# Six modulation pairs of two column strips each in place of twelve single units

## The reference, cut to what matters

```
mod_lat = silu(c) @ w_mod + b_mod          # w_mod: 1024 x 6144
mod_ctx = silu(c_ctx) @ w_mod + b_mod
sh1, sc1, g1, sh2, sc2, g2 = split(mod_lat, 6)
prj_c = modulate(rmsnorm(ctx), sh1c, sc1c) @ w_in
prj_l = modulate(rmsnorm(x),   sh1,  sc1)  @ w_in
...
x = x + g1 * mix_l
x = x + g2 * hier_moe(modulate(rmsnorm(x), sh2, sc2), ...)
```

## Time and profile before

| what | us |
|---|---|
| median of three runs | 1448.57 |
| the runs | 1447.49, 1448.57, 1452.31 |
| span of the profiled execution, first to last instruction | 1448.4 |
| TensorE busy in it | 1317.8 (91%) |
| VectorE busy | 800.7 (55%) |
| ScalarE busy | 612.3 (42%) |
| GpSimd busy | 85.0 (6%) |

### The profile page before, as it was taken

One profiled execution on the slowest core, in us unless ns is written; L12 is line 12 of the kernel. 1 busy time (PEld: TensorE's weight loads), 2 busy tenths in 40 slices (PEclk: granted clock), 3 DMA queues, 4 the chain that ended last, 5 costly groups with the idle time before them and its releaser, 6 DMA issues.

```text
span 1448.4 us, 26402 instructions
## 1 busy us (share of the span) xinstructions
PE 1317.8 (91%) x11218; PEld 1122.8 (78%) x11218; DVE 800.7 (55%) x1221; ACT 612.3 (42%) x952; POOL 85.0 (6%) x65
## 2 busy tenths in 40 slices
PE   7999999999999999999999999899978767877877
PEld 7989798999989988899998999688545333444534
DVE  5557846776467676877548797785212111221314
ACT  6553346434466676455446654764211111111112
POOL 2000000000002200321001000320000000000000
PEclk9999999999999999999999999999999998999999
DMA  9654346454474585444554060349999999999996
GB/s 372 245 210 182 117 175 274 188 202 180 175 289 177 188 326 227 190 175 175 188 204 200 2 253 12 161 168 382 403 427 427 430 428 429 428 427 429 425 428 269
DMA packets 30358, 383.31 MB, mean 265 GB/s; under 512 B 3552, under 2 KB 3728, under 8 KB 7216
## 3 DMA queue, kind: packets, MB, share of 16 engines
q1 hardware_dynamic: 29504, 377.72, 64.3%
q0 software_dynamic: 752, 4.11, 0.7%
HBM read 380.77 MB, written 1.05 MB: 264 GB/s over the span
## 4 chain that ended last, share of the span: by engine, by line
PE 55%; DMA 25%; DVE 11%; ACT 5%; issue 2%; SPq 0%; POOL 0%; DVEq 0%; ACTq 0%; POOLq 0%
PE ps L688 55%; DMA ring<-in_experts 25%; DVE w_lo L2002 3%; DVE work L2014 2%; ACT work L1453 2%; ACT w_hi L1453 2%; DVE work L2002 1%; DVE HM L2002 1%; ACT L1453 1%; DVE act L2002 1%; ACT HM L1453 1%; ACT act L1453 0%; DVE HM L2008 0%; DVE work L2281 0%; PE ps L837 0%
## 5 line engine op out<-in xcount | busy, mean ns | idle before, releaser
L2002 DVE TENSOR_TENSOR w_lo<-ring,w_hi 128x1024 fp32r<-128x1024 f32 (+1 forms) x273 | 342.0, 1262 | 209.5 <-ACT w_hi L1453 209.0
L688 PE MATMUL ps<-in_hi,w_hi 128*128 128x256 f32 x1376 | 391.2, 284 | 15.0 <-DVE w_lo L2002 14.1
L688 PE MATMUL ps<-in_hi,w_lo 128*128 128x256 f32 x1376 | 387.3, 281 | 0.0
L688 PE MATMUL ps<-in_lo,w_hi 128*128 128x256 f32 x1376 | 387.0, 281 | 0.0
L1453 ACT ACTIVATE w_hi<-ring 128x1024 fp32r<-128x1024 f32 (+1 forms) x273 | 286.3, 1053 | 234.1 <-PE ps L688 230.4
L688 PE MATMUL ps<-ring,work 128*32 128x256 f32 (+3 forms) x2520 | 201.3, 452 | 85.5 <-DMA ring<-in_experts 77.7
L688 PEld LDWEIGHTS ps<-in_hi,w_hi 128*128 128x128 f32 x1376 | 261.5, 190 | 20.4 <-issue 16.6
L688 PEld LDWEIGHTS ps<-in_lo,w_hi 128*128 128x128 f32 x1376 | 261.5, 190 | 0.3
L688 PEld LDWEIGHTS ps<-in_hi,w_lo 128*128 128x128 f32 x1376 | 261.4, 190 | 0.0
L688 PEld LDWEIGHTS ps<-ring,work 128*32 128x32 f32 (+1 forms) x2520 | 83.8, 117 | 185.8 <-issue 103.8
L2014 DVE SCALAR_TENSOR_TENSOR X<-ps,mod,X 128x256 f32<-128x256 f32 x136 | 59.0, 479 | 249.4 <-PE ps L688 249.3
(11 more groups left out here) (291 smaller groups left out, 1904.0 us busy)
## 6 DMA issues: line engine op xcount, KB each, us to landing
ring<-in_experts SPq DMA_DIRECT2D x89, 2048.0 KB, 23.1
ring<-in_dense SPq DMA_DIRECT2D x82, 2048.0 KB, 7.7
ring<-in_experts SPq DMA_DIRECT2D x5, 512.0 KB, 21.5
work<-in_experts SPq DMA_DIRECT2D x1, 2048.0 KB, 12.6
ring<-in_dense SPq DMA_DIRECT2D x3, 512.0 KB, 7.4
spare<-in_experts SPq DMA_DIRECT2D x1, 1536.0 KB, 10.9
cst<-in_ret_cst POOLq DMA_DIRECT2D x1, 1280.0 KB, 12.6
cst<-in_experts SPq DMA_DIRECT2D x1, 1280.0 KB, 5.7
```

Of the source, the lines that this page charges most:

```text
L688: i = pe.matmul(o, l, r, start=start, stop=stop)
L2002: i = dve.tensor_tensor(out=o, in0=x, in1=y, op=op)
```

## The change

The twelve units become six pairs (`MOD_GROUPS`). A pair's 16 matmuls go to the four strips of one bank: unit one to strips 0 and 1, unit two to strips 2 and 3, each strip summing four input blocks. The order alternates so that four matmuls in a row go to strips 0, 1, 2, 3. Both units must have landed before the first matmul; the first unit's slot is released near the pair's end. ScalarE reads one bank per pair. A fold is again four matmuls, each with four moving columns (two per unit), so it serves both units.

The first pair (units 0 and 1) is done at the retention's end, with its fold now between the two halves of head 3's transposes. Pairs 1, 2 and 4 are at the starts of `ffn_in0`, `lru_u` and `ffn_in1`. Nothing is left inside the recurrent gates; pair 3 follows them, with its fold behind the first unit of `lru_out`. Pair 5 is at `ctx_b`. The stream of loads is put in the same order. With six tiles fewer, the bank of each later tile is counted anew, and the expert stage takes its bank numbers from the tiles.

```diff
-STREAM = [("ret_g", 0, 4), ("ret_v", 0, 4), ("ret_q", 0, 2), ("ret_k", 0, 2), ("mod", 0, 1), ("ret_out", 0, 4),
-          ("mod", 1, 2), ("ffn_in0", 0, 11), ("ffn_out0", 0, 6), ("mod", 3, 2), ("lru_u", 0, 3), ("lru_y", 0, 3),
-          ("lru_gate", 0, 1), ("mod", 5, 1), ("lru_gate", 1, 1), ("mod", 6, 2), ("lru_out", 0, 3), ("mod", 8, 2), ("ffn_in1", 0, 11),
+STREAM = [("ret_g", 0, 4), ("ret_v", 0, 4), ("ret_q", 0, 2), ("ret_k", 0, 2), ("mod", 0, 2), ("ret_out", 0, 4),
+          ("mod", 2, 2), ("ffn_in0", 0, 11), ("ffn_out0", 0, 6), ("mod", 4, 2), ("lru_u", 0, 3), ("lru_y", 0, 3),
+          ("lru_gate", 0, 2), ("mod", 6, 2), ("lru_out", 0, 3), ("mod", 8, 2), ("ffn_in1", 0, 11),
...
+MOD_GROUPS = (0, 1), (2, 3), (4, 5), (6, 7), (8, 9), (10, 11)
...
 for _i in range(KL):
-    if _i == KL // 2:
-        _mod(5)
     _seq.append(("lru_gate", _i))
-_mod(6, 7)
+_mod(3)
...
-GATHER_BANK, Y_BANK = 2, 4
-SCATTER_BANKS = 5, 6, 7, 3
+GATE_BANK, UP_BANK, GATHER_BANK, _last = (TILE["t_tok", i] % ROT for i in range(4))
+Y_BANK = GATHER0[1]
+SCATTER_BANKS = GATHER0[0], STAT, MODB, _last
...
+            def mod_rows(group):
+
+                units = MOD_GROUPS[group]
+                w = weights("mod", units[0]), ring[SLOT[UNIT_AT["mod", units[1]]]]
+                await_unit(pe, UNIT_AT["mod", units[1]])
+                if group == 0:
                     pe.wait_ge(s["csil_ready"], 1)
+                t = TILE["mod", group]
                 await_room(pe, t)
+                for first in range(0, KD, 2):
+                    for n in range(2):
+                        for c in (first, first + 1):
+                            rows = slice((2 * n + c % 2) * STRIP, (2 * n + c % 2 + 1) * STRIP)
+                            mm(bank(t)[rows, :], csil[:, c, :], w[n][:, c * 512:(c + 1) * 512], c < 2, c >= KD - 2,
+                               bank_full[t % ROT] if n and c == KD - 1 else None)
+                        if n == 0 and first == KD - 2:
+                            left.append(slot_used[SLOT[UNIT_AT["mod", units[0]]]])
...
+                to = cut(ps[:, MODB, 8 * units[0]:8 * (units[0] + 2)], 2, 8)
+                fold = cut(col("fold", 0, 4), 2, 2)
                 for m in range(4):
+                    mm(to[:, :, 2 * m:2 * m + 2], act2[:, group % 2, m * P:(m + 1) * P], fold, True, True,
                        s["mod_full"] if m == 3 else None)
...
+                    if h == HEADS - 1 and tau == 0:
+                        mod_cols(0)
...
-                            (values, 2), (turn_head, 1), (values, 3), (mod_rows, 0), (turn_head, 2), (mod_cols, 0),
-                            (turn_head, 3)):
+                            (values, 2), (turn_head, 1), (values, 3), (mod_rows, 0), (turn_head, 2), (turn_head, 3)):
...
-                if n == 2:
-                    mod_rows(5)
-                if n == 4:
-                    mod_cols(5)
-            mod_rows(6)
-            mod_rows(7)
-            mod_cols(6)
+            mod_rows(3)
...
                 if n == 0:
-                    mod_cols(7)
+                    mod_cols(3)
...
             root(0)
-            mod_read(5)
             gate_tiles(3)
             decays(1)
             gate_tiles(4)
             gate_tiles(5)
-            mod_read(6)
             decays(2)
-            mod_read(7)
+            mod_read(3)
```

More of the change, by code:

```diff
@@ L88 @@
         ("norm2", KD), ("final", KD), ("c", 2 * KD), ("b_route", NR), ("dt_bias", 1), ("a_log", 1),
-        ("eps", 1), ("desc", NJ), ("steps", T // CAP), ("forward", 1), ("backward", 1), ("fold", 2)]
+        ("eps", 1), ("desc", NJ), ("steps", T // CAP), ("forward", 1), ("backward", 1), ("fold", 4)]
 VOFF, _n = {}, 0
@@ L150, with _mod @@
 _tiles("k", 4)
-def _mod(*units):
-    _seq.extend(("mod", i) for i in units)
+MOD_GROUPS = (0, 1), (2, 3), (4, 5), (6, 7), (8, 9), (10, 11)
+def _mod(group):
+    _seq.append(("mod", group))
 for _kind, _h in (("s", 0), ("s", 1), ("o", 0), ("s", 2), ("o", 1), ("t", 0), ("s", 3), ("o", 2), ("t", 1), ("o", 3),
@@ L161 @@
 _tiles("ret_out", 4)
-_mod(1, 2)
+_mod(1)
 _tiles("ffn_in0", 2 * KF // 2)
 _tiles("ffn_out0", 4)
-_mod(3, 4)
+_mod(2)
 _tiles("lru_u", KL // 2)
@@ L168 @@
 for _i in range(KL):
-    if _i == KL // 2:
-        _mod(5)
     _seq.append(("lru_gate", _i))
-_mod(6, 7)
+_mod(3)
 _tiles("lru_out", 4)
-_mod(8, 9)
+_mod(4)
 _tiles("ffn_in1", 2 * KF // 2)
 _tiles("ffn_out1", 4)
-_mod(10, 11)
+_mod(5)
 TURN_LAG = 2
@@ L228 @@
 GATHER0 = [TILE["route", 0] % ROT, TILE["route", 1] % ROT]
-GATHER_BANK, Y_BANK = 2, 4
-SCATTER_BANKS = 5, 6, 7, 3
+GATE_BANK, UP_BANK, GATHER_BANK, _last = (TILE["t_tok", i] % ROT for i in range(4))
+Y_BANK = GATHER0[1]
+SCATTER_BANKS = GATHER0[0], STAT, MODB, _last
 WARM_END = 5
 WARM = 6
-LAST_Y_BANKS = Y_BANK, GATHER_BANK, 0, 1
-assert GATHER0 == [5, 4]
+LAST_Y_BANKS = Y_BANK, GATHER_BANK, GATE_BANK, UP_BANK
+assert sorted((GATE_BANK, UP_BANK, GATHER_BANK, Y_BANK) + SCATTER_BANKS) == list(range(8))
 def two_blocks(nc, a, out):
@@ L773, in outer_gemm, with mod_cols @@
                     after(c)
-            def mod_rows(i):
-                w = weights("mod", i)
-                if i == 0:
+            def mod_rows(group):
[3 more added lines that the diff above has]
+                if group == 0:
                     pe.wait_ge(s["csil_ready"], 1)
-                t = TILE["mod", i]
+                t = TILE["mod", group]
                 await_room(pe, t)
[L782 to L790, removed]
+                for first in range(0, KD, 2):
[6 more added lines that the diff above has]
+                            left.append(slot_used[SLOT[UNIT_AT["mod", units[0]]]])
+            def mod_cols(group):
+                units = MOD_GROUPS[group]
+                await_read(pe, TILE["mod", group])
+                to = cut(ps[:, MODB, 8 * units[0]:8 * (units[0] + 2)], 2, 8)
+                fold = cut(col("fold", 0, 4), 2, 2)
                 for m in range(4):
-                    n = 2 * (4 * i + m)
-                    mm(ps[:, MODB, n:n + 2], act2[:, i % 2, m * P:(m + 1) * P], col("fold", 0, 2), True, True,
+                    mm(to[:, :, 2 * m:2 * m + 2], act2[:, group % 2, m * P:(m + 1) * P], fold, True, True,
                        s["mod_full"] if m == 3 else None)
@@ L814, in output_sums, with next_input @@
                        s["stats_full"] if c == KD - 1 else None)
-            def next_input(i, name, units):
+            def next_input(i, name, groups):
                 if i:
@@ L820, in next_input @@
                     output_sums(i - 1)
-                for u in units:
+                for u in groups:
                     mod_rows(u)
@@ L912, in _ @@
             ffn(0)
-            next_input(2, "lru_u", (3, 4))
+            next_input(2, "lru_u", (2,))
             split_gemm("lru_u", KL, KD, in_hi, in_lo, first_m=BPC)
@@ L960, in _ @@
                 if n == 0:
-                    mod_cols(7)
-            next_input(3, "ffn_in1", (8, 9))
+                    mod_cols(3)
+            next_input(3, "ffn_in1", (4,))
             ffn(1)
@@ L1384, in one_pair @@
                     for half in range(2):
-                        i = pe.transpose(ps[:, 0, half * P:(half + 1) * P], hs[:, half * P:(half + 1) * P], ident[:, :])
+                        i = pe.transpose(ps[:, GATE_BANK, half * P:(half + 1) * P], hs[:, half * P:(half + 1) * P], ident[:, :])
                     i.then_inc(s["ht_full"], 1)
@@ L1613, in _ @@
             mixer_out("ret_out", lambda j: weights_hi(chunks_by("ret_out", j)))
-            next_input(1, "ffn_in0", (1, 2))
+            next_input(1, "ffn_in0", (1,))
             def context_hi(j):
@@ L2839, in _layout @@
     put("backward", (np.arange(ND) >= SH).astype(np.float32)[:, None], ND)
-    put("fold", (np.arange(P)[:, None] % STRIP == np.arange(2)).astype(np.float32))
+    put("fold", ((np.arange(P)[:, None] % STRIP == np.arange(4) % 2) & (np.arange(P)[:, None] // 64 == np.arange(4) // 2)).astype(np.float32))
     ret, ssd, glob = _constants()
```

31 lines of the change are left out of this document (14 added, 17 removed).

## The result

The changed kernel takes 1440.98 us, the median of seven runs (1439.53 to 1447.53); seven runs of the kernel before, taken beside them, have 1450.90. The ratio is 0.9939, 95% interval 0.9926 to 0.9953: by the ratio 8.9 us faster, by the two medians 9.9. The forecast was 4.8 us faster, 1443.8; its range ended 0.8 us above the result. The profiled execution took 1440.12 us.

The account below looks back on a forecast made before the run. The prediction took TensorE as the bound up to 1033 us, then mostly expert loads waiting for slots it frees. Terms 1.83 + 0.92 + 0.92 + 0.97 + 0 + 0.18 = 4.8 us, from 1448.57 to 1443.8; range 1441.8 to 1448.0.

Parts of the forecast that it names:

- (a): Rival at the retention's end: the clock falls there anyway; price 1.83 us, 1445.6 us in all; chance 0.18.
- (c): Rival at ffn_in0 and lru_u: VectorE and ScalarE set the pace there too; 1.84 us less, 1445.6 us; chance 0.09.
- (b): Rival in the recurrent part: the clock falls because TensorE idles 1.8 and 2.0 us; 1.3 us lost, 1445.1; chance 0.11.
- The fold's price: At every site: a fold pass costs 0.115 us with four moving columns too, so a saved fold is worth 0.92 us.
- ffn_in0 and lru_u: At the start of both stages: TensorE is on the path, so the saved fold gives 0.92 us each.
- (e): Rival, slower: a pair's strips run two side by side instead of four, 3.6 us more a pair; 1457 us; chance 0.05.
- The retention's end: A second unit's strips fill TensorE's 1.67 us gap and the clock stays up: gain 1.83 us, capped by VectorE.
- The recurrent gates: Two strip reads of 0.48 and 0.49 us leave ScalarE's chain: gain 0.97 us.
- a sign that the prediction itself gave of being wrong: The prediction is wrong if a clock of 0.50 stands at the retention's end or in the recurrent part.
- ffn_in1: At its start: gain 0, as TensorE waits for VectorE's low parts, some 4 us instead of 3.2.
- ctx_b: TensorE comes to the statistics 0.92 us earlier and waits for GpSimd's sum: gain 0.18 us.
- "Should arrive at the end undiminished": Time saved ahead of the expert weight loads reaches the kernel's end in full, since each load waits for a TensorE-freed slot.

## Why the prediction was right, and where it was not

Faster was right, by 8.9 us instead of 4.8, and four fifths of it or more came from a thing that the prediction does not contain. That is luck: by themselves the edits are worth 2.2 us by the two spans, less than half of the sum, below the 4.3 us that the prediction takes as what can be told from no change, and not to be seen in total times. Its range is also added wrongly at the upper end: with (a)'s 1.83 and (c)'s 1.84 gone and (b)'s 1.3 lost, 1443.8 becomes 1448.7, not 1448.0. Its sum and the measured parts, against the kernel before at the same layout:

- **The fold's price** held: 0.95 us and eight passes wherever it stands. Against the Trainium skill's charge for small matmuls (TensorEngine Tiling, Instruction Overhead), the row of the trace was the better price here too.
- **ffn_in0 and lru_u**, 0.92 each: 0.89 and 0.89, undone by the two folds of two columns. Rival (c) is out. The strips take 3.64 us a pair in each place, so (e) is out.
- **The retention's end**, 1.83: every event came as described, but the term was mis-sized, 0.1 to 0.3. It priced the low clock of one execution, 0.50 all through 173 to 177 us. With the gap as it was, the kernel with two unused columns has 0.50 for half as long, and the 37th matmul of ret_out starts at 176.41 us, only 0.27 behind VectorE's last low part; with the pairs it starts at 176.13. So VectorE all but sets the pace there, and little is left to gain. Two more profiles of the old order (the two with all sets at one difference) have the low clock about as short. Rows of the kernel with two unused columns:

```profile
171.00:173.00 2.00, 2.00 (x11) 2.00 (x10) 1.90 (x4) 1.23 (x2) 0.00 (x0) 0.50 0.94 279
173.00:177.00 4.00, 4.00 (x31) 4.00 (x30) 3.65 (x6) 2.82 (x4) 0.00 (x0) 0.84 0.95 401
```

- **The recurrent gates**, 0.97: 0.98 arrives at lru_out's first low part, and 0.48 of it is lost in the next five chunks, where the clock stands at 0.57 over 527 to 531 us. So rival (b) came, at a good third of its price of 1.3, and with it a sign that the prediction itself gave of being wrong, a low clock in this place. In five of the seven profiled kernels with this order the clock fell once between 511 and 531 us, in none of the five with the old one; the other two have the same gaps, 2.3 and 1.7 to 1.8 us.
- **ffn_in1**, 0: TensorE waits 3.9 us for low parts instead of 3.2, as said; 0.2 came all the same. **ctx_b**, 0.18: 0.14, behind GpSimd's sum as said.
- **"Should arrive at the end undiminished"** failed: between ssd_xs and mix_out 1.07 us went. The filled gap lost 1.05 in the same place, and there the two kernels with all sets at difference 192 moved by 2.4 us against each other, though in different modes. The low clock stands at other instructions in each of these traces; which chance puts it there was not tried, so the cause stays open.
- **The step that failed** is the pricing of the widened `fold`. The prediction counted its four columns as moving columns and stopped. That the constant array grows by two numbers, and that what lies behind it moves by 32 bytes, has no term in it; it was worth 7.9 us, more than all the edits together. Of the sum itself, the retention's end is the term that was furthest off, 0.3 instead of 1.83.

## What to carry to other kernels

Compare the distance of like matmuls in stretches that a change does not touch before crediting the change: a count over 100 us is enough, and an unused column or two in the array of constants gives a kernel of the same layout to compare with. Give an effect that hangs on the clock in one profiled execution the width that several executions show. When weights change with every matmul, choose the addresses of weights and moving operands on purpose, by their difference, and time several executions, since two of the differences have two spacings.

## What the hardware showed that was not expected

- The spacing of 128x256 products with new weights each time depends on the difference of the two operands' addresses modulo 256 bytes: 113.3 to 120.1 ns in steps of 32 bytes, with no load and no other engine at work. Over the kernel, 32 bytes more gave 7.9 us, and the next 32, in the changed kernel, brought it to 5.9 us over the kernel before.
- At differences of 192 and 64 there are two spacings, 113.3 and 117.8 ns, and TensorE can keep the one it is in for whole stages. At 192, three matmuls at difference 0 straight ahead brought it to 113.3 in all eight cases, 24 in all eight, and a chunk of them in 56 of 59 cases in the changed kernel; at 64 they did not.
- TensorE's clock fell to 0.50 behind idle gaps of 1.7 to 2.3 us in some profiled kernels and not in others with the same order and the same gaps, for stretches of unequal length. Filling the gap of 1.67 us kept it up; with one of the two later gaps filled, it fell behind the other.
